# Moving the last convolution steps and their norm under the up projections, and the compressed scores' mask a round ahead, in a two-layer transformer block kernel

## The reference, cut to what matters

```python
proj = h @ w_in[l]
a_q, a_kv, a_gate, d_q, d_kv, b_in, c_in = jnp.split(proj, splits, axis=-1)
o_cmp, p_cmp = nsa_compressed_attention(qa, k_cmp, v_cmp)        # softmax over 15 compressed keys, masked
o_slc = nsa_selected_attention(qa_rot, ...)                      # branch 0 is the gated sum of o_cmp,
o_win = banded_attention(qa_rot, ...)                            #   o_slc and o_win
o_b = conformer_conv(b_in, ...)                                  # branch 1
o_c = pool_mixer(c_in, ...)                                      # branch 2
o_d = banded_attention(qd, ...)                                  # branch 3
up = jnp.einsum("bsnc,ncd->bsnd", branches, w_branch[l])
gates = jax.nn.sigmoid((h @ w_gate[l]).reshape(bsz, seq, N_BRANCH, D_MODEL))
mix = jnp.einsum("bsnd,bsnd->bsd", gates, up) @ w_o[l]
x = x + rms_norm(mix, norm_mix_post[l])
# then a feed-forward part, and x again

def conformer_conv(u, conv_w, conv_b, ln_g, ln_b):
    a, gte = jnp.split(u, 2, axis=-1)
    c = a * jax.nn.sigmoid(gte)
    c = causal_depthwise_conv(c, conv_w, conv_b)                 # 31 taps, 512 channels
    return jax.nn.silu(layer_norm(c, ln_g, ln_b))
```

## Time and profile before

| | us |
|---|---|
| median of 3 runs | 1848.98 |
| lowest, highest | 1848.62, 1851.53 |
| the profiled execution | 1848.22 |
| its span (first to last instruction) | 1846.1 |

### The profile page before, as it was taken

One profiled execution on the slowest core, in us unless ns is written; L12 is line 12 of the kernel. 1 busy time (PEld: TensorE's weight loads), 2 busy tenths in 40 slices (PEclk: granted clock), 3 DMA queues, 4 the chain that ended last, 5 costly groups with the idle time before them and its releaser, 6 DMA issues. The chain is left out here.

```text
span 1846.1 us, 26665 instructions
## 1 busy us (share of the span) xinstructions
PE 1681.4 (91%) x10712; PEld 1382.2 (75%) x10712; DVE 1094.0 (59%) x1490; ACT 761.3 (41%) x1071; POOL 338.1 (18%) x321
## 2 busy tenths in 40 slices
PE   7988879899998998979899997999898988999996
PEld 6887779699986887779799983445475537899995
DVE  4677987656645667887556631274547335355555
ACT  4354554455533354554455521213125323343431
POOL 0222213135301222213134300013320000000000
PEclk9998989999999998989899999999968997899998
DMA  6544435466563534435466554221100132355551
GB/s 253 201 162 160 183 117 198 156 237 231 185 214 138 200 143 163 180 133 187 148 229 237 186 193 160 81 87 69 46 23 1 49 134 92 123 186 182 187 182 74
DMA packets 40122, 282.07 MB, mean 153 GB/s; under 512 B 4816, under 2 KB 5072, under 8 KB 6864
## 3 DMA queue, kind: packets, MB, share of 16 engines
q1 hardware_dynamic: 38432, 273.15, 41.0%
q10 hardware_dynamic: 1584, 7.42, 1.2%
HBM read 279.50 MB, written 1.05 MB: 152 GB/s over the span
## 5 line engine op out<-in xcount | busy, mean ns | idle before, releaser
L430 DVE TENSOR_TENSOR ring_low<-ring,sb_hi 128x2048 fp32r<-128x2048 f32 (+1 forms) x116 | 246.9, 2129 | 203.2 <-ACT sb_hi L423 203.2
L423 ACT ACTIVATE sb_hi<-ring 128x2048 fp32r<-128x2048 f32 x116 | 222.5, 1918 | 294.8 <-DMA ring<-weights 124.4
L582 PE MATMUL psum<-sb_hS,sb_hi 128*128 128x256 f32 x704 | 203.8, 290 | 6.5 <-DVE ring_low L430 6.5
L1843 DVE TENSOR_TENSOR sb_split<-ring,sb_split 128x2048 fp32r<-128x2048 f32 x48 | 109.9, 2292 | 153.4 <-ACT sb_split L1838 153.4
L585 PE MATMUL psum<-sb_hS,sb_hi 128*128 128x256 f32 x704 | 200.5, 285 | 0.0
L586 PE MATMUL psum<-sb_hS,ring_low 128*128 128x256 f32 x704 | 199.5, 283 | 0.0
L841 PE MATMUL psum<-sb_hfT,ring_low 128*128 128x256 f32 x704 | 197.8, 281 | 0.0
L2157 PE MATMUL psum<-sb_hfS,sb_split 128*128 128x256 f32 x512 | 146.6, 286 | 5.9 <-DVE sb_hfS L2687 3.9
L582 PEld LDWEIGHTS psum<-sb_hS,sb_hi 128*128 128x128 f32 x704 | 135.2, 192 | 15.9 <-DVE ring_low L430 8.9
L2160 PE MATMUL psum<-sb_hfS,sb_split 128*128 128x256 f32 x512 | 145.9, 285 | 0.0
L2161 PE MATMUL psum<-sb_hfS,sb_split 128*128 128x256 f32 x512 | 145.8, 285 | 0.0
(11 more groups left out here) (393 smaller groups left out, 3981.5 us busy)
## 6 DMA issues: line engine op xcount, KB each, us to landing
ring<-weights SPq DMA_DIRECT2D x256, 1024.0 KB, 4.8
sb_rows_ffn<-rows ACTq DMA_DIRECT2D x4, 512.0 KB, 4.4
sb_rows_mix<-rows ACTq DMA_DIRECT2D x2, 1024.0 KB, 5.1
sb_rows<-rows ACTq DMA_DIRECT2D x1, 2048.0 KB, 8.9
sb_x<-x_in SPq DMA_DIRECT2D x2, 512.0 KB, 5.9
sb_y<-ctx_in SPq DMA_DIRECT2D x1, 1024.0 KB, 5.9
out<-sb_x SPq DMA_DIRECT2D x2, 512.0 KB, 2.7
sb_const<-const SPq DMA_DIRECT2D x1, 711.0 KB, 13.7
```

Of the source, the lines that this page charges most:

```text
L423: act.activation(hi_of(n), ring[:, c % SLOTS, :], ACT.Copy).then_inc(hi_ready, 1)
L430: eng.tensor_tensor(low_of(n)[:, half], ring[:, SPLIT_CHUNKS[n] % SLOTS, half], hi_of(n)[:, half].bitcast(F32), ALU.subtract)\
L582: mm = pe.matmul(out, hi[:, k, bs], hS[:, 0, k, :], start=(k == 0), stop=False)
L1843: dve.tensor_tensor(split[:, n % SPLITS, 1, :], ring[:, (first_moe + n) % SLOTS, :], split[:, n % SPLITS, 0, :].bitcast(F32), ALU.subtract ...
```

## The change

Seven moves, in both layers:

- The compressed scores' mask (`cmp_mask`) goes from round 1 to round 0 on DVE, ahead of that round's 12 convolution steps, and `cmp_exps` to the end of round 0 on ACT.
- The two `cpT` jobs become one: PE waits for both halves and turns both, ACT copies both at once, between the gate's copy and the next high part.
- Of the 40 convolution steps, 8 stay ahead of the low part of the first up chunk and 6 ahead of that of the second; the others go between the up steps: 3 after the first product of a chunk, 5 after its second and the low part that follows, and all that are left after chunk 2.
- PE turns the convolution ahead of up step (0, 3) (`CONV_BEFORE`) instead of ahead of all up steps; `conv_norm` on DVE and `conv_roots` on POOL go with it.
- The normalised part is turned ahead of up steps (3, 1) and (3, 2) instead of (0, 2) and (3, 0).
- ACT makes the high parts of up chunks 4 and 5 ahead of the first half's activation, that of chunk 6 ahead of the second's.
- The low part of the convolution's output comes after product (3, 2) instead of (3, 1).

```diff
+CONV_BEFORE = (0, 3)
-OB_BEFORE = {(0, 2): 0, (3, 0): 1}
+OB_BEFORE = {(3, 1): 0, (3, 2): 1}
...
         def cmp_out():
-            for t in range(TT):
-                pe.wait_ge(cmp_p, t + 1)
-                transpose4(("cpT", t), [csc[:, t, :]])
+            pe.wait_ge(cmp_p, TT)
+            transpose4("cpT", [csc[:, t, :] for t in range(TT)])
...
-        for t in range(TT):
-            pe.wait_ge(conv_done, 4 * TAPS)
-            transpose4(("convT", t), [acc[:, b, t * P:(t + 1) * P] for b in range(4)])
+        def conv_turns(n, i):
+
+            if (n, i) == CONV_BEFORE:
+                for t in range(TT):
+                    pe.wait_ge(conv_done, 4 * TAPS)
+                    transpose4(("convT", t), [acc[:, b, t * P:(t + 1) * P] for b in range(4)])
+            if (n, i) in OB_BEFORE:
+                t = OB_BEFORE[(n, i)]
+                jobs.wait_drained(pe, ("convT", t))
+                transpose4(("obT", t), [ln_tm[:, t, b * P:(b + 1) * P] for b in range(4)])
...
                 for i in range(2):
+                    conv_turns(n, 2 * half + i)
                     name = ("up", n, 2 * half + i)
...
-        def gate_step():
+        def gate_step(between=None):
 
             gate_out(1)
+            if between is not None:
+                between()
             gate_hi()
...
                 exps(r, 0)
-                if r == 1:
-                    cmp_exps()
                 exps(r, 1)
-            gate_step()
+            gate_step(cmp_copy if r == 1 else None)
...
             gate_step()
+            if r == 0:
+                cmp_exps()
...
-        split_hi(act, FIRST_UP + 2)
-        split_hi(act, FIRST_UP + 3)
+        for n in range(FIRST_UP + 2, FIRST_UP + 6):
+            split_hi(act, n)
         for t in range(TT):
-            split_hi(act, FIRST_UP + 4 + t)
+            if t == 1:
+                split_hi(act, FIRST_UP + 6)
             jobs.wait_filled(act, ("obT", t))
...
-            if r == 1:
-                cmp_mask()
             split_lo(dve, FIRST_GATE + 2 * r + 1)
...
+            if r == 0:
+                cmp_mask()
             conv_steps(12)
         split_lo(dve, FIRST_GATE + 15)
         out_low(len(ROUNDS) - 1)
-        conv_steps(4 * TAPS)
+        conv_steps(8)
         split_lo(dve, FIRST_UP)
...
+        conv_steps(6)
         split_lo(dve, FIRST_UP + 1)
+
+        def conv_norm():
...
                 jobs.drain(dve.tensor_tensor(dst, jobs.out(name), g2, ALU.mult), name)
-                if i % 2 == 1:
+                if (n, i + 1) == CONV_BEFORE:
+                    conv_norm()
+                if (n, i + 1) == (3, 3):
...
+                if i % 2 == 0:
+                    conv_steps(3)
+                else:
                     chunk = 2 * bi + i // 2
...
                     if chunk < 7:
                         split_lo(dve, FIRST_UP + chunk + 2)
+                    conv_steps(5 if chunk < 2 else 4 * TAPS)
...
+                if (n, i + 1) == CONV_BEFORE:
+                    conv_roots()
```

More of the change, by code:

```diff
@@ L255, in plan_layer @@
         jobs.plan(("cs", t), ("u", "t")[t])
-    for t in range(TT):
-        jobs.plan(("cpT", t), "u")
+    jobs.plan("cpT", "u")
     for a, t in ROUNDS:
@@ L263, in plan_layer @@
         jobs.plan(("modT", i), "t")
-    for t in range(TT):
-        jobs.plan(("convT", t))
     for n in BRANCH_ORDER:
         for i in range(4):
+            if (n, i) == CONV_BEFORE:
+                for t in range(TT):
+                    jobs.plan(("convT", t))
             if (n, i) in OB_BEFORE:
@@ L737, in values @@
                 jobs.wait_drained(pe, "kc")
-                jobs.wait_drained(pe, ("cpT", t))
+                jobs.wait_drained(pe, "cpT")
                 for j in range(4):
@@ L1063, in scalar_program @@
         load_rows(act, "post_mix", 2 * D, mem["rows_mix"][:, :, :].rearrange("p i c -> p (i c)"), mix_rows_in)
-        for n in range(FIRST_UP + 6, FIRST_WO + 1):
+        for n in range(FIRST_UP + 7, FIRST_WO + 1):
             split_hi(act, n)
@@ L1392, in vector_program @@
         out_low(len(ROUNDS) - 1)
-        conv_steps(4 * TAPS)
+        conv_steps(8)
         split_lo(dve, FIRST_UP)
[L1397 to L1405, removed]
-        split_lo(dve, FIRST_UP + 1)
+        conv_steps(6)
+        split_lo(dve, FIRST_UP + 1)
+        def conv_norm():
+            for t in range(TT):
+                jobs.wait_filled(dve, ("convT", t))
+                order.up(dve.bn_stats(stats[:, t, :], jobs.out(("convT", t))))
+                order.here(dve)
+                dve.bn_aggr(mv[:, t, :], stats[:, t, :]).then_inc(stat_ready, 1)
+            for t in range(TT):
+                dve.wait_ge(lnstd_ready, t + 1)
+                jobs.drain(dve.tensor_scalar(ln_tm[:, t, :], jobs.out(("convT", t)), mv[:, t, 0:1], lnstd[:, t:t + 1],
+                                             ALU.subtract, ALU.mult), ("convT", t))
         def mix_low(i):
@@ L1430, in vector_program @@
                 jobs.drain(dve.tensor_tensor(dst, jobs.out(name), g2, ALU.mult), name)
-                if i % 2 == 1:
-                    chunk = 2 * bi + i // 2
[L1433 to L1438, removed]
+                if (n, i + 1) == CONV_BEFORE:
+                    conv_norm()
+                if (n, i + 1) == (3, 3):
+                    for t in range(TT):
+                        dve.wait_ge(ob_hi, t + 1)
+                        part = brS[1][:, :, :, t * P:(t + 1) * P]
+                        dve.tensor_tensor(part[:, 1, :, :], acc[:, :, t * P:(t + 1) * P], part[:, 0, :, :].bitcast(F32),
+                                          ALU.subtract).then_inc(ob_lo, 1)
+                if i % 2 == 0:
+                    conv_steps(3)
+                else:
+                    chunk = 2 * bi + i // 2
                     if chunk < 7:
                         split_lo(dve, FIRST_UP + chunk + 2)
+                    conv_steps(5 if chunk < 2 else 4 * TAPS)
                     if chunk == 6:
@@ L1557, in gpsimd_program, with conv_roots @@
             pool.wait_ge(lo_pool, n - POOL_LOWS[0] + 1)
[L1559 to L1563, removed]
+        def conv_roots():
+            for t in range(TT):
+                pool.wait_ge(stat_ready, t + 1)
+                chain(pool.tensor_scalar(msq[:, 2:3], mv[:, t, 1:2], 1.0, EPS, ALU.mult, ALU.add))
+                pool.tensor_tensor(lnstd[:, t:t + 1], msq[:, 2:3], K("mhalf", 0, 1), ALU.pow).then_inc(lnstd_ready, 1)
+                pool.wait_ge(lnstd_ready, t + 1)
         k = 0
```

5 lines of the change are left out of this document (2 added, 3 removed).

## The result

The changed kernel took 1838.12 us (median of 4 runs, 1835.78 to 1839.51), the kernel before 1849.85 (1848.62 to 1851.53) beside it: a ratio of 0.9935, 95% interval 0.9917 to 0.9952. That is 12.0 us faster, between 8.9 and 15.4. The prediction was faster, 1841.5 in 1833 to 1846: the direction and the range hold, the centre is 3.4 us too slow. The profiled execution took 1839.51 us with a span of 1837.5, 8.6 less than before.

A forecast was written before the change was run, and what follows sets the result against it. DVE was taken to set the time at the gates' end, PE after it. Rounds -10.2 us and the convolution's part +0.8 and +1.9 gave -7.5 from a median of 1848.98: 1841.5 us, range 1833 to 1846.

The forecast's parts named there:

- Part 1: Mask and copy of the compressed scores, first round: gate 3 starts 5.1 us earlier, -10.2 us over two layers.
- Part 2: Convolution under the up projections: PE's wait moves to up step (0, 3), branch 1 starts 0.8 and 1.9 us later.
- the Trainium skill's rule: VectorE and GpSimd instructions block each other for a whole instruction: 2.7 us instead of 2.5 for POOL's additions beside steps.
- three prices for POOL: POOL's two additions for branch 0 delay the convolution steps by 2.5 us, taken between bounds of 0 and 2.7.
- The sum: Over both layers, -10.2 us for the rounds, +0.8 and +1.9 for the convolution's part, together -7.5 us.
- Case (a): Under the up projections, POOL's additions fall beside other instructions: branch 1 3.4 and 2.3 us earlier, 1833; chance 0.17.
- Case (c): No change: a low part comes late in each up chunk, 3.3 us a layer, sum -0.9, 1848; chance 0.13.
- Case (d): Slower: the convolution's norm is late before branch 1, 9.7 us of lateness a layer, 1853 or more; chance 0.05.
- Case (b): Convolution done when PE arrives at its turning: branch 1 11.7 and 10.6 us earlier, 1816.5; chance 0.05.

The follow-up runs named there:

- the two runs apart: Each against the kernel before: the mask a round sooner alone, 1843.18 us (ratio 0.9965); the one copy alone, 1838.43 us (0.9936).
- the run with the convolution alone: Only the convolution's steps, turning and norm moved under the up projections, compressed scores as in the kernel before: 1850.06 us, ratio 1.0003.
- the runs of the two parts alone: Against the kernel before: only the moves of round 1 (mask and copy), 1837.82 us (ratio 0.9941); only the convolution's part, 1850.06 us (1.0003).
- the last experiment: The version of 1815.87 us with the normalised convolution turned one up step earlier, ahead of (3, 0) and (3, 1): 1818.12 us, ratio 0.9826.
- the run with the steps in DVE's waits: The changed kernel with 15 of the last 40 convolution steps put into waits that DVE has anyway: 1825.08 us, ratio 0.9872.
- the run before it: The changed kernel with 15 last steps in DVE's waits and round 0's 12 steps moved behind round 1's weights: 1815.87 us, ratio 0.9811.

## Why the prediction was right

**Part 1** said 5.1 us a layer and the trace shows 5.30, with the steps as foretold: no wait for the mask, one wait of 5.81 on the weights, which end when they did, and the two transposes behind it. It didn't say that the mask's move is worth nothing beside the copy's; the two runs apart show it, and its own argument (DVE does the same work in another order) contains it. It took the clock to fall as it did; it fell, but not for as long: after the earlier gate 3, layer 1 loses 1.5 us up to the gates' end, layer 2 nothing. In layer 1 the low clock lasts until 148.7, 3.3 us into gate 3 (before, until 150.6, 1.6 us into it), which is half of that, 0.76 us; in layer 2, after the same wait of 5.81, it lasts 1.2 us. The other 0.75 us lie behind a later wait that the change doesn't touch, ahead of a step of the modulation. It is as long in all four cases, but PE goes on from it at either clock, first in the two layers before, then in the two after:

```profile
203.47 1.07 PE L498 MATMUL psum<-ring,sb_cvec 128*32 128x512 f32 x8 [3.27 <-DVE sb_modT L1159]
...
756.07 1.93 PE L498 MATMUL psum<-ring,sb_cvec 128*32 128x512 f32 x8 [3.25 <-DVE sb_modT L1159]
```

```profile
200.60 1.93 PE L499 MATMUL psum<-ring,sb_cvec 128*32 128x512 f32 x8 [3.27 <-DVE sb_modT L1166]
...
747.99 1.06 PE L499 MATMUL psum<-ring,sb_cvec 128*32 128x512 f32 x8 [3.27 <-DVE sb_modT L1166]
```

The same eight matmuls take 1.07 us at the higher clock and 1.93 at the lower, and which it is changes between the layers of one execution. So this part of the loss can't be put down to the change.

**Part 2** said that a wait of 8.8 us would stand ahead of up step (0, 3), and there it stands with 8.24. The sum was +0.8 and +1.9 us for the two layers, 2.7; the trace has -0.06 and +0.82. Term by term in layer 1: PE starts the up steps 0.95 us late (1.0 said); POOL takes 2.0 us from the steps (2.5 said); from the turning to up step (0, 3) it is 1.62 us (1.9 said); that step takes 3.83, 1.0 over 2.83 (1.2 said); branch 1 waits 1.27 (1.5 said). Each was a little too dear, by 1.3 us together; the up steps took 0.2 us more than said ahead of the turning and 0.3 behind it, so branch 1 comes 0.9 sooner than forecast. The part's true price of about 0.8 us agrees with the 0.6 of the run with the convolution alone. The estimate of 2.7 by the Trainium skill's rule was the dearest of the three prices for POOL: it counts both additions in full, and here the second was itself held up for most of DVE's low part.

**The sum** was -7.5. The table's lines that the change touches give -8.4 (-5.30, +1.51, -0.06, -5.40, +0.05, +0.82), the runs of the two parts alone -10.3 (-10.9 and +0.6), the ratio of the runs -12.0, of which the interval leaves 8.9 at the near end. The term that was mis-sized is Part 2, by 2 us. Of the other 2.5 us no step shows the place; the executions of the changed kernel lie up to 3.7 us apart, and the profiled one is the longest of them.

**The rivals.** Case (a), lighter cover, was the nearest miss on the fast side: the additions did fall beside the steps. Case (c) did not come: the only wait of the up steps on a low part is the 0.95 at their start. Case (d) did not come either, no PE wait on the norm's values, but the last experiment brings it about by asking for them 2.84 us sooner. Case (b), all hidden, needed DVE to be done when PE arrives; with 11 steps moved into the last round and 4 more ahead of the first up chunk, that is what happened.

## What to carry to other kernels

Work that is moved under another engine's stage is hidden only if its own engine has free time there ahead of the moment of need: count that engine's queue, with every wait in it, up to that moment, before counting the wait as won. Idle time to fill is the moved engine's own, so look for the places where it waits itself (here 11 steps put into the last round gave some 7.5 us, and the same 40 steps spread under the up projections gave nothing). And two waits in a row on one chain don't add up: take each away alone before taking the credit for both.

## What the runs showed that was not expected

Idle time and the clock did not go together simply. After 1.27 us of idle PE ahead of branch 1 in the changed kernel the clock stayed at its higher level; after 2.19 us at the same place, with the convolution's steps done early, it fell to the lower one for 3 us; after 3.28 us ahead of the normalised part's turning it stayed high. In the first case the first up step of branch 1 took 2.89 us. The second case is a row of that step in the run with the steps in DVE's waits, where it took 4.35; the third is the row at 287.75 above:

```profile
303.30 0.41 PE L800 MATMUL psum<-sb_br,sb_hi 128*128 128x256 f32 x1
```

A matmul of this form takes 0.28 us at the higher level and 0.41 at the lower. Nor does the place settle it. In layer 2 of the last experiment the same turning behind the same wait took 1.09 us at the low clock (the row at 825.43) instead of 0.63. In the run before it the 2.19 us ahead of branch 1 left the clock low in layer 1 and high in layer 2, and the wait of 3.27 us on `sb_modT` shows both in one execution. The runs show that the length of a wait and its place do not fix the clock behind it; what does, they leave open.

This bears on single rows. After 9.59 us of wait the first up step took 4.63 us in layer 1 and 3.53 in layer 2 of the kernel before; after 8.24 us, up step (0, 3) took 3.83 in the changed kernel, and after 6.23 us 4.83. So a microsecond of wait that is saved need not be a microsecond of time, and a microsecond lost or won behind one wait in one execution is not yet a price.
